# Attention heads transposed in the last projection step, into the tiles of query and key, and retention heads inside the first output unit

## The reference

```python
def hybrid_mixer(h, w_in, w_out, pos):
    proj = h @ w_in
    rq, rk, rv, rg, aq, ak, av = jnp.split(proj, offsets, axis=-1)
    ...
    ret = head_group_norm(retention_chunkwise(rq, rk, rv)).reshape(B, S, RET_HEADS * RET_DV)
    ret = jax.nn.silu(rg) * ret
    ...
    att = dilated_mixture(aq, ak, av).reshape(B, S, ATT_HEADS * ATT_DH)
    return jnp.concatenate([ret, att], axis=-1) @ w_out

def reference(x, ...):
    x = x + hybrid_mixer(rms_norm(x, norm_mix_g[l]), w_in[l], w_out[l], pos)
    x = x + moe_ffn(rms_norm(x, norm_ffn_g[l]), w_router[l], b_router[l], ...)
    return rms_norm(x, norm_final_g)
```

## Time and profile before

| | us |
|---|---|
| three runs | 1457.61, 1456.10, 1455.11 |
| median | 1456.10 |
| profiled execution | 1457.89 |
| its span | 1456.1 |
| TensorE busy in the span | 1392.3 (96%) |
| VectorE, ScalarE, GpSimd busy | 1232.9, 1024.3, 407.4 |
| mean granted clock of TensorE | 0.981 |

### The profile page before, as it was taken

The page is one execution under the profiler, slowest core; times in us unless marked ns, Lnnn a source line. Parts: engine busy times, 40 slices in busy tenths (PEclk is TensorE's granted clock), DMA queues, the critical chain, the costliest instruction groups (busy, mean ns, idle before and its releaser), DMA issues.

```text
span 1456.1 us, 19517 instructions
## 1 busy us (share of the span) xinstructions
PE 1392.3 (96%) x6520; PEld 1155.7 (79%) x6520; DVE 1232.9 (85%) x927; ACT 1024.3 (70%) x750; POOL 407.4 (28%) x231
## 2 busy tenths in 40 slices
PE   6999998967999999999999999999999999999995
PEld 5877886856888888888888888888888888888874
DVE  5534546266999999999999999999999999999986
ACT  5234333255888888888888888888888888888874
POOL 0000000176363333333333333333333333333311
PEclk9999998968999999999999999999999999999998
DMA  8221324346999999999999999999999999999993
GB/s 304 94 75 59 101 73 115 122 171 234 360 389 385 382 383 384 383 385 380 370 371 382 380 381 369 386 382 381 380 381 381 382 386 384 384 383 382 374 337 123
DMA packets 81017, 453.48 MB, mean 311 GB/s; under 512 B 13887, under 2 KB 13903, under 8 KB 32736
## 3 DMA queue, kind: packets, MB, share of 16 engines
q1 hardware_dynamic: 68968, 432.55, 75.1%
q0 software_dynamic: 10304, 18.26, 4.9%
q10 hardware_dynamic: 1720, 2.34, 0.5%
HBM read 447.63 MB, written 22.59 MB: 323 GB/s over the span
## 4 chain that ended last, share of the span: by engine, by line
PE 85%; DMA 4%; DVE 3%; POOL 3%; issue 2%; ACT 2%; SPq 0%; ACTq 0%; DVEq 0%; POOLq 0%
PE ps L1703 14%; PE ps L1708 14%; PE ps L1704 14%; PE ps L1666 7%; PE ps L1668 7%; PE ps L1674 7%; PE ps L1397 4%; PE ps L1398 4%; PE ps L1403 4%; DMA acc_rows<-y,idx_scatter 2%; PE ps L1644 2%; PE ps L1657 2%; POOL slot_table L604 1%; ACT whi L686 1%; POOL idx_scatter L594 1%
## 5 line engine op out<-in xcount | busy, mean ns | idle before, releaser
L979 DVE TENSOR_TENSOR wlo<-raw,whi 128x2048 fp32r<-128x2048 f32 x274 | 648.7, 2389 | 109.5 <-ACT whi L686 109.1
L686 ACT ACTIVATE whi<-raw 128x2048 fp32r<-128x2048 f32 x274 | 520.8, 1914 | 141.3 <-PE ps L1708 91.6
L1703 PE MATMUL ps<-whi,xT_hi 128*128 128x512 f32 x992 | 390.6, 394 | 8.3 <-ACT ps L841 8.3
L1704 PE MATMUL ps<-whi,xT_lo 128*128 128x512 f32 x992 | 387.3, 390 | 0.0
L1708 PE MATMUL ps<-wlo,xT_hi 128*128 128x512 f32 x992 | 266.4, 390 | 0.0
L1703 PEld LDWEIGHTS ps<-whi,xT_hi 128*128 128x128 f32 x992 | 187.2, 189 | 47.2 <-issue 8.7
L1708 PEld LDWEIGHTS ps<-wlo,xT_hi 128*128 128x128 f32 x992 | 186.8, 188 | 38.9
L1704 PEld LDWEIGHTS ps<-whi,xT_lo 128*128 128x128 f32 x992 | 187.1, 189 | 38.0
L1666 PE MATMUL ps<-whi,actT_hi 128*128 128x512 f32 x496 | 195.9, 395 | 0.0
L1668 PE MATMUL ps<-whi,actT_lo 128*128 128x512 f32 x496 | 193.2, 390 | 0.0
L594 POOL COPY idx_scatter<-tab 128x1 uint32 (+1 forms) x31 | 59.2, 1910 | 321.6 <-ACT y L828 321.6
(11 more groups left out here) (223 smaller groups left out, 1652.0 us busy)
## 6 DMA issues: line engine op xcount, KB each, us to landing
raw<-in_w_gate_up SPq DMA_DIRECT2D x130, 1024.0 KB, 8.8
raw<-in_w_down SPq DMA_DIRECT2D x126, 1024.0 KB, 9.6
raw_a<-in_w_gate_up SPq DMA_DIRECT2D x63, 1024.0 KB, 7.0
raw_b<-in_w_gate_up SPq DMA_DIRECT2D x63, 1024.0 KB, 7.5
raw<-in_w_in SPq DMA_DIRECT2D x14, 1024.0 KB, 5.2
raw<-in_w_out SPq DMA_DIRECT2D x4, 1024.0 KB, 4.9
x<-in_x SPq DMA_DIRECT2D x4, 512.0 KB, 8.1
acc_rows<-x SPq DMA_DIRECT2D x4, 512.0 KB, 4.8
```

What stands on the lines that cost most here:

```text
L686: nc.scalar.activation(whi_slot(n), raw_slot(slot_of(n)), ACT.Copy).then_inc(hi_done, 1)
L979: nc.vector.tensor_tensor(wlo_slot(n), raw_slot(slot_of(n)), whi_slot(n).bitcast(F32), ALU.subtract).then_inc(lo_done, 1)
L1703: mm(ps[:, part, :], xT_hi[:, u, :], w_hi_ap, start=False, stop=False, skip_group_check=True)
L1704: mm(ps[:, part, :], xT_lo[:, u, :], w_hi_ap, start=False, stop=False, skip_group_check=True)
```

## The change

Four things are changed together; no arithmetic is.

1. The attention heads get transposed tiles of their own, `attT_hi` and `attT_lo`, where `qT` and `kT` lay (query and key, last read by `ret_scores` in step 53). `cat_part(q)` gives a head's two parts, and retention heads now have indices 0 to 3 in `catT_hi` and `catT_lo`.
2. Each head of a half has its own bank, 4 to 7. TensorE transposes heads 0 to 2 after step 54, head 3 between the high and the low products of step 55; retention heads 4 and 5 after chunk 2 of unit 14, 6 and 7 after chunk 3. The `ready` waits ask for one head at a time in the first chunk of units 14 and 15.
3. ScalarE and VectorE make copies and subtractions of the attention heads in step 55; the root of the group norm comes before the copy of unit 16, the sum for it before the last gate product.
4. GpSimd's router loads also wait until the 14 projection units are used, since heads 0 to 3 are now transposed before the projection ends.

```diff
+    attT_hi, _ = place(area + 32 * K, "attT_hi", [H, S], F32R)
+    attT_lo, _ = place(area + 40 * K, "attT_lo", [H, S], F32R)
...
+    def cat_part(q):
+
+        return (attT_hi[:, q, :], attT_lo[:, q, :]) if q < H else (catT_hi[:, q - H, :], catT_lo[:, q - H, :])
...
             pl.wait_ge(c_tr, H)
+            pl.wait_ge(used, U_OUT)
...
+            def cat_hi(q):
+
+                act_e.wait_ge(c_tr, q + 1)
+                nc.scalar.activation(cat_part(q)[0], ps[:, 4 + q % H, :], ACT.Copy).then_inc(c_hi, 1)
...
+                if b == 8 * NG - 1:
+                    for q in range(H - 1):
+                        cat_hi(q)
                 if RET + 2 <= b < RET + 2 + H:
                     act_e.wait_ge(r_pv, b - RET - 1)
                     h = b - RET - 2
                     nc.scalar.activation(cat_ret[:, :, h * DH:(h + 1) * DH],
                                          ps[:, 7, :].rearrange("p (c d) -> p c d", c=NC), ACT.Copy).then_inc(r_copy, 1)
+                if b == 8 * NG - 1:
+                    cat_hi(H - 1)
...
-            for h in range(H):
-                act_e.wait_ge(c_tr, h + 1)
-                nc.scalar.activation(catT_hi[:, H + h, :], ps[:, 6 + h % 2, :], ACT.Copy).then_inc(c_hi, 1)
-            hi(16)
             act_e.wait_ge(gn_var, 1)
             nc.scalar.activation(small[:, 9, :], small[:, 8, :], ACT.Sqrt).then_inc(gn_root, 1)
-            for h in range(H):
-                act_e.wait_ge(c_tr, H + h + 1)
-                nc.scalar.activation(catT_hi[:, h, :], ps[:, 4 + h % 2, :], ACT.Copy).then_inc(c_hi, 1)
+            hi(16)
+            for q in range(H, 2 * H):
+                cat_hi(q)
...
+            def cat_lo(q):
+
+                v.wait_ge(c_hi, q + 1)
+                nc.vector.tensor_tensor(cat_part(q)[1], ps[:, 4 + q % H, :], cat_part(q)[0].bitcast(F32),
+                                        ALU.subtract).then_inc(c_lo, 1)
...
+                if b == 8 * NG - 1:
+                    for q in range(H - 1):
+                        cat_lo(q)
                 if RET + 3 <= b < RET + 3 + H:
                     head_stats(b - RET - 3)
+                if b == 8 * NG - 1:
+                    cat_lo(H - 1)
+                    head_stats(H - 1)
+                    nc.vector.tensor_copy(small[:, 14, :], mv[:, :, 0])
+                    nc.vector.tensor_scalar(small[:, 8, :], mv[:, :, 1], EPS, None, ALU.add).then_inc(gn_var, 1)
...
-            head_stats(H - 1)
-            for h in range(H):
-                v.wait_ge(c_hi, h + 1)
-                nc.vector.tensor_tensor(catT_lo[:, H + h, :], ps[:, 6 + h % 2, :], catT_hi[:, H + h, :].bitcast(F32),
-                                        ALU.subtract).then_inc(c_lo, 1)
-
-
-            nc.vector.tensor_copy(small[:, 14, :], mv[:, :, 0])
-            nc.vector.tensor_scalar(small[:, 8, :], mv[:, :, 1], EPS, None, ALU.add).then_inc(gn_var, 1)
...
+            for q in range(H, 2 * H):
+                cat_lo(q)
             lo(16)
-            for h in range(H):
-                v.wait_ge(c_hi, H + h + 1)
-                nc.vector.tensor_tensor(catT_lo[:, h, :], ps[:, 4 + h % 2, :], catT_hi[:, h, :].bitcast(F32),
-                                        ALU.subtract).then_inc(c_lo, 1)
...
+                    if ready:
+                        ready(k)
                     w_hi_ap, _ = unit_part(n, k)
                     mm(out_ap, x_hi_of(k), w_hi_ap, start=opened and k == 0, stop=False)
                     mm(out_ap, x_lo_of(k), w_hi_ap, start=False, stop=False)
+                if between:
+                    between()
...
+                                  between=(lambda: transpose_cat(H - 1)) if b == 8 * NG - 1 else None)
...
+            def transpose_cat(q):
+
+                src = cat_att if q < H else cat_ret
+                if q == 0:
+                    pe.wait_ge(a_out, NC * H)
+                    pe.wait_ge(r_st, H)
+                if q == H - 1:
+                    pe.wait_ge(r_copy, H)
+                if q >= H:
+                    pe.wait_ge(c_lo, q - H + 1)
+                    pe.wait_ge(r_cat, q - H + 1)
+                h = q % H
+                for c in range(NC):
+                    last = nc.tensor.transpose(ps[:, 4 + h, c * P:(c + 1) * P], src[:, c, h * DH:(h + 1) * DH], ident)
+                last.then_inc(c_tr, 1)
...
+                if b == 8 * NG - 2:
+                    for q in range(H - 1):
+                        transpose_cat(q)
...
-                if c == 0:
-                    pe.wait_ge(c_lo, H if (part == 0) else 2 * H)
-                k0 = KU * (1 - part)
-                last = unit_chunk(n, ps[:, c, :], lambda k: catT_hi[:, k0 + k, c * P:(c + 1) * P],
-                                  lambda k: catT_lo[:, k0 + k, c * P:(c + 1) * P], c == 0, part == 0, part == 1)
+                last = unit_chunk(n, ps[:, c, :], lambda k: cat_part(H * part + k)[0][:, c * P:(c + 1) * P],
+                                  lambda k: cat_part(H * part + k)[1][:, c * P:(c + 1) * P], c == 0, part == 0, part == 1,
+                                  ready=(lambda k: pe.wait_ge(c_lo, H * part + k + 1)) if g == 0 and c == 0 else None)
                 finish(last, part == 1, c == NC - 1)
 
             for c in range(NC):
                 out_project(U_OUT, c)
-            for q in range(H, 2 * H):
-                transpose_cat(q)
+                if c >= 2:
+                    transpose_cat(2 * c)
+                    transpose_cat(2 * c + 1)
```

## The result

The changed kernel takes 1445.97 us (median of 4 runs, 1445.31 to 1446.56), the kernel before 1456.31 beside it (4 runs, 1455.11 to 1457.61): a ratio of 0.9924, interval 0.9912 to 0.9935, or 10.3 us less (9.5 to 12.8 by the interval). The time is 1.1 over the forecast of 1444.9 and inside the range. The profiled execution took 1446.0 with a span of 1444.2, 11.9 under the span of 1456.1 before.

A forecast was written before the change was run, and what follows sets the result against it. TensorE was bound by work, except two holes with low clock behind them. Free time 5.98 and 2.92 plus clock 1.41 and 1.47, less 0.42 stall and 0.16 operation changes, gave 11.2 off 1456.1: 1444.9 us, range 1442.3 to 1448.9.

The forecast's parts named there:

- the two holes: TensorE's gaps from attention transposes to unit 14 (224.03 to 231.77, 7.74 us) and retention transposes to unit 15 (4.68 us).
- The new order on TensorE: From 221.21, TensorE's reordered transposes and products bring unit 15's chunk 1 to 241.74 in place of 252.94, 11.20 us less.
- The clock: First chunks of units 14 and 15 at full clock take 2.72 us each, saving 1.41 and 1.47.
- The holes' own part: Free time around the attention and retention transposes, beyond the 1.76 us of transposes in each: 5.98 and 2.92 us.
- changes of operation: On TensorE, 0.08 us added wherever transposes give way to multiplications; 0.16 us added in all.
- The stall: In unit 15's chunk 0, TensorE stands 0.42 us until the last retention head's subtraction at 240.37.
- The covers: Time by which feeding steps precede TensorE's need: retention copy 0.4, head 3's subtraction 0.9, gated heads 2.0, 0.8, 2.2, 0.9 us.
- Other queues: Later weight-unit copies and subtractions, GpSimd's router loads near 226 and gain row near 237: nothing is paid.
- Rival 1, a cover short: Retention chain or a copy comes late and TensorE stands with it: 1446.9 to 1448.3 us; chance 12%.
- Rival 2, the clock: The clock still falls behind unit 15's stall, chunk 0 costing 1.47 us more: 1446.4 us; chance 7%.
- Rival 3, the expert stage: First expert's 16 stores meet VectorE's subtractions differently: up to 18.9 us more, 1463.8, or at best 1436.6; chance 5%.
- My step of one store: In the first expert's stage, an expected shift of about one GpSimd slot-table store, 2 us, either way.

The follow-up runs named there:

- the filler in the kernel before: The kernel before, with no head moved and products nobody reads put into TensorE's idle time around the attention and retention transposes; 1454.5 us, ratio 0.9981.
- the late copy: The changed kernel with three idle ScalarE copies ahead of the retention copy of head 3; 1446.92 us, ratio 0.993 to the kernel before.
- Root late: The changed kernel with the group norm's root behind the copy of weight unit 16 on ScalarE again; 1446.92 us, ratio 0.9929 to the kernel before.
- attention back: The changed kernel with all four attention heads transposed after the last projection step again, tiles and four banks kept; 1449.34 us, ratio 0.9943 to the kernel before.
- retention back: The changed kernel with retention heads transposed after unit 14 again, in two banks by turns and with the old waits; 1448.78 us, ratio 0.994 to the kernel before.
- the earlier broadcast: The changed kernel with head 6 transposed inside unit 14's chunk 3 and expert 1's two bias broadcasts ahead of the last four stores; 1439.96 us, ratio 0.9882.

## Why the prediction was right, step by step

- **What bounds.** TensorE is at its limit outside the two holes: right. All of 11.22 that the stretch gives reaches the end of the profiled execution (11.9 with 0.51 and 0.21 from behind). That the rest moved so little is luck in part: in the same kernel run again the third column is 2.92 longer (1089.15, 1092.07), and that execution ends 2.1 later.
- **The new order on TensorE.** With 0.15 added for the later start, the forecast was 221.36, 224.58, 226.01, 234.17, 237.85, 238.73 and 241.89; the rows read 221.44, 224.61, 225.98, 234.17, 237.78, 238.58 and 241.87. The sum was 11.20, the trace gives 11.22.
- **The terms.** The clock was put at 1.41 + 1.47 = 2.88 of it; the filler in the kernel before measures 2.62 (2.58 in the two chunks). The holes' own part, less stall and changes of operation, 8.32, is then 8.6. The terms are off by 0.3 against each other, and the sum comes out to 0.02 because these errors cancel.
- **The stall** of 0.42 in unit 15's chunk 0: 238.58 to 240.96 is 2.38 for eight products that take 1.82 + 0.08, so 0.48. It isn't one stop but two late pairs, the third and the fourth.
- **The covers.** Retention copy 0.4: measured 0.47 in the rows, 0.54 by the late copy. Subtraction of head 3, 0.9: it ends at 226.63, wanted at 227.36, 0.73. Gated heads ready at 232.13, 233.89, 235.64 and 237.39 for transposes at 234.17, about 234.6, 237.78 and about 238.2: 2.0, 0.7, 2.1, 0.8, against 2.0, 0.8, 2.2, 0.9. The root ended at 229.06 (forecast 228.9 + 0.15), its table load began at 227.55 (227.4 + 0.15) with no wait. Root late: a delay of 1.80 less the second head's cover of 0.7 gave the wait of 1.07.
- **Other queues.** Unit 16's and 17's subtractions run from 240.25 to 244.83 (forecast 240.3 to 245), GpSimd's router load at 226.76 (near 226), the gain row at 237.69 (near 237), VectorE's use of the router weights at 244.75 (near 245). Nothing is paid at any of them.
- **Rival 1, a cover short:** did not come; the late copy and the late root show what it would have cost, 1.1 and 1.3.
- **Rival 2, the clock:** did not come. Idle time of 0.64 and 1.66 in one kernel, and of 0.48 in pieces in the other, left the granted clock at 1.00; 2.50 in one piece (attention back) and 0.98 + 1.50 with transposes between (retention back) brought it to 0.62 and 0.64. One trace of each would prove little, since behind the last expert's wait the same kernel shows either level. But at this place the ten traces that have only a small stall of 0.3 to 0.5 in unit 15's chunk 0 all show 1.00 there. By these rows the rule that the prediction took from the Trainium skill, "TensorE: Matmul & The Clock Gate", section "A second HAM failure mode: psum-queue depth-cycling", is not borne out for the small stalls of this kernel.
- **Rival 3, the expert stage:** it moved by 0.51, where I had left 2 either way. The reason I gave, that both queues start from the same point, is only half of it: stores beside a subtraction wait for its end, and eight of them do so before and after. My step of one store, 2 us, was of the right kind and too long: a store that slips costs 1.3, and in four of the traces one does. The term's other end, TensorE's 8.3 of waiting to be had, was real in part: the earlier broadcast takes some 4 from the stage.
- **From the profiled execution to the median.** This is where the 1.1 over the forecast lies. I took 11.2 off a median of 1456.1; the medians differ by 10.3 (1456.31 to 1445.97) and by 10.0 in the other set of runs (1457.14 to 1447.14). The intervals, 9.5 to 12.8 and 9.0 to 13.0, hold 11.2. That the difference is the third column's scatter is argued from the table, not shown: it would take profiles of every timed run.

## To carry over

When one engine is full outside a few holes, write its new order out with the time per instruction from its own timeline, give every feeding step a cover in microseconds, and the stretch can come out to a tenth, as here, where terms that were off by 0.3 cancelled; the covers also say in advance which part of the edit could be left out. Price the clock apart from the hole that brings it down, with products nobody reads, and look next at who waits behind a queue that only happens to be in the way, like a broadcast behind stores. Judge edits of 1 us by distances between two fixed points in a trace, not by medians.

## What the runs showed of the hardware, not expected

GpSimd's casts of the router constants, 0.29, 0.29 and 0.19 before (from 246.91), now meet VectorE's weight subtractions; GpSimd's timeline of the kernel after:

```profile
242.64 2.35 POOL L553 CAST ones_r<-cst 128x128 fp32r<-128x128 f32 x1
```

One cast of 128 x 128 took 2.35, eight times its length, and ended 0.16 after VectorE's subtraction (240.25 + 4.58 = 244.83); the cast before it took 0.61 and ended 0.16 after the first of the two subtractions in that row. Broadcasts do the same: 1.30 alone, 3.16 and 3.46 beside subtractions (with the bias earlier, at 322.13 and 325.16), and the linear one ended 1.15 behind the subtraction of 325.18 + 2.29 = 327.47. The Trainium skill, "SBUF — State Buffer", section "SBUF: two separate sides", has the port of the two engines as an exclusive lock, held against a GpSimd operation that reads SBUF by a VectorE operation with two SBUF inputs; the subtraction has two, the cast reads, and the rows agree. It cost nothing here, since the casts have 40 us until the router's tables.

The clock of the last expert falls or stays from one execution to the next, with the same program (8.06 behind a wait of 2.14, 9.67 behind one of 2.84), and over all traces the length of the wait doesn't order the outcomes. And both bias broadcasts ahead of four stores made the group of 16 stores shorter, 25.8 in place of 29.5, by taking the stretches beside VectorE in their stead.
